# Ninety-six token slots per expert in place of 128, with 128-column stationary operands kept

## The reference, cut to what matters

```python
D_MODEL = 1024; SEQ = 256; D_FF = 3584; N_EXPERTS = 8; TOP_K = 2

def moe_ffn(h, router, w_gate_up, w_down):
    B, S, D = h.shape
    t = h.reshape(B * S, D)
    logits = (t @ router).astype(jnp.float32)
    top_v, top_i = lax.top_k(logits, TOP_K)
    gates = jax.nn.softmax(top_v, axis=-1)
    combine = jnp.sum(jax.nn.one_hot(top_i, N_EXPERTS, dtype=jnp.float32) * gates[..., None], axis=1)
    out = jnp.zeros_like(t)
    for e in range(N_EXPERTS):
        out = out + combine[:, e:e + 1].astype(t.dtype) * swiglu(t, w_gate_up[e], w_down[e])
    return out.reshape(B, S, D)
```

## Time and profile before

| | |
|---|---|
| median of 3 runs | 1419.13 us (1418.8 to 1419.32) |
| span of the profiled execution | 1417.7 us |
| TensorE busy | 1411.1 us (100% of the span), 6721 matmuls |
| TensorE weight loads | 1185.2 us (84%) |
| VectorE busy | 1234.8 us (87%) |
| ScalarE busy | 964.5 us (68%) |
| GpSimd busy | 101.9 us (7%) |
| HBM traffic | 442.93 MB, 312 GB/s over the span |

### The profile page before, as it was taken

One profiled execution on the slowest core, in us unless ns is written; L12 is line 12 of the kernel. 1 busy time (PEld: TensorE's weight loads), 2 busy tenths in 40 slices (PEclk: granted clock), 3 DMA queues, 4 the chain that ended last, 5 costly groups with the idle time before them and its releaser, 6 DMA issues.

```text
span 1417.7 us, 19898 instructions
## 1 busy us (share of the span) xinstructions
PE 1411.1 (100%) x6721; PEld 1185.2 (84%) x6721; DVE 1234.8 (87%) x1207; ACT 964.5 (68%) x840; POOL 101.9 (7%) x147
## 2 busy tenths in 40 slices
PE   9999999999999999999999999999999999999999
PEld 8998888888988888888888888888888888888887
DVE  6486888878677898999989999999999999999887
ACT  7465544443694677777777777787777777777775
POOL 4010000000022020010010000001001000000000
PEclk9999999999999999999999999999999999999999
DMA  9554655564445799999999999999999999999995
GB/s 321 163 180 147 219 196 178 178 204 144 127 177 194 274 384 389 375 378 393 379 382 394 374 374 396 394 374 382 393 371 382 395 382 374 395 383 382 383 393 195
DMA packets 212592, 442.93 MB, mean 312 GB/s; under 512 B 16372, under 2 KB 56760, under 8 KB 212544
## 3 DMA queue, kind: packets, MB, share of 16 engines
q1 hardware_dynamic: 208640, 430.18, 83.0%
q0 software_dynamic: 3888, 12.13, 2.9%
q10 hardware_dynamic: 16, 0.00, 0.0%
HBM read 434.88 MB, written 7.37 MB: 312 GB/s over the span
## 4 chain that ended last, share of the span: by engine, by line
PE 98%; ACT 1%; DVE 1%; issue 0%; POOL 0%; ACTq 0%; DVEq 0%; POOLq 0%
PE PS L1729 21%; PE PS L1730 21%; PE PS L1733 21%; PE PS L1431 5%; PE PS L1430 5%; PE PS L1432 5%; PE PS L1162 3%; PE PS L1218 2%; PE PS L1210 2%; PE PS L1212 2%; PE PS L1269 1%; PE PS L1275 1%; PE PS L1272 1%; PE PS L1718 1%; PE PS L1192 1%; PE PS L1721 1%
## 5 line engine op out<-in xcount | busy, mean ns | idle before, releaser
L1884 DVE TENSOR_TENSOR wlo<-ring,whi 128x2048 fp32r<-128x2048 f32 x334 | 758.8, 2290 | 53.3 <-ACT whi L799 51.2
L799 ACT ACTIVATE whi<-ring 128x2048 fp32r<-128x2048 f32 x334 | 639.8, 1918 | 184.3 <-PE PS L1733 173.8
L1729 PE MATMUL PS<-whi,xhi 128*128 128x512 f32 x864 | 340.8, 394 | 0.0
L1730 PE MATMUL PS<-whi,xlo 128*128 128x512 f32 x864 | 336.6, 390 | 0.0
L1733 PE MATMUL PS<-wlo,xhi 128*128 128x512 f32 x864 | 231.0, 389 | 0.0
L1733 PEld LDWEIGHTS PS<-wlo,xhi 128*128 128x128 f32 x864 | 162.1, 188 | 34.0 <-DVE wlo L1884 0.2
L1730 PEld LDWEIGHTS PS<-whi,xlo 128*128 128x128 f32 x864 | 162.4, 188 | 32.4
L1729 PEld LDWEIGHTS PS<-whi,xhi 128*128 128x128 f32 x864 | 162.3, 188 | 32.4
L1729 PE MATMUL PS<-whi,hhi 128*128 128x512 f32 x440 | 171.4, 389 | 0.0
L1730 PE MATMUL PS<-whi,hlo 128*128 128x512 f32 x440 | 171.2, 389 | 0.0
L1733 PE MATMUL PS<-wlo,hhi 128*128 128x512 f32 x440 | 117.8, 390 | 0.0
(11 more groups left out here) (387 smaller groups left out, 1637.1 us busy)
## 6 DMA issues: line engine op xcount, KB each, us to landing
ring<-in_moe_w_gate_up SPq DMA_DIRECT2D x448, 512.0 KB, 6.7
ring<-in_moe_w_down SPq DMA_DIRECT2D x224, 512.0 KB, 7.2
ring<-in_dense_w_gate_up SPq DMA_DIRECT2D x56, 512.0 KB, 4.6
ring<-in_dense_w_down SPq DMA_DIRECT2D x28, 512.0 KB, 4.1
ring<-in_a_w_in SPq DMA_DIRECT2D x12, 768.0 KB, 8.6
ring<-in_mem_w_kv SPq DMA_DIRECT2D x4, 1024.0 KB, 7.7
ring<-in_a_w_out SPq DMA_DIRECT2D x4, 1024.0 KB, 5.3
ring<-in_b_w_out SPq DMA_DIRECT2D x4, 1024.0 KB, 7.3
```

Of the source, the lines that this page charges most:

```text
L799: nc.scalar.activation(whi[:, j, :], ring[:, h * SLOT:(h + 1) * SLOT], ACT.Copy).then_inc(S("highs"), 1)
L1729: mm(out_, lhsT=xh, rhs=whi[:, j, c0:c0 + HD], start=begin, stop=False)
L1730: mm(out_, lhsT=xl, rhs=whi[:, j, c0:c0 + HD], start=False, stop=False)
L1884: v.tensor_tensor(wlo[:, j, :], ring[:, h * SLOT:(h + 1) * SLOT], whi[:, j, :].bitcast(F32), ALU.subtract).then_inc(S("lows"), 1)
```

## The change

`CAP` becomes 96, so a pass gives each expert 96 slots and `PASSES` becomes 3. The stationary operands of the matmuls stay 128 columns wide: they are read through `wide_` and `hhiW`/`hloW`, patterns that take the 96 slots and the 32 columns behind them, and write all 128 partitions of the accumulators, of which 96 are then read. Everything else that goes by slots becomes 96 wide: the moving identity of the transposes, the one-hot gather, the hidden splits, the row fetches and adds, and the squares of `turn_rows` (12 in place of 16, three per block). The placing of slots gets a step for a third pass.

```diff
-CAP = 128
+CAP = 96
...
-        Sx = carve(o, NT, CAP); o += NT * CAP
+        Sx = carve(o, NT, P); o += NT * P
...
-        xe_ = slice(0, CAP)
+        xe_, wide_ = slice(0, CAP), slice(0, P)
+        hhiW, hloW = ([bass.AP(h.tensor, h.offset + c * CAP, [list(h.ap[0]), [1, P]]) for c in range(4)] for h in (hhiE, hloE))
...
-            pool.tensor_copy(blank[:, :, 1], iota[0:NC + 1]).then_inc(S("iota"), 1)
+            pool.tensor_copy(blank[:, :, 1], iota[0:NC + 1, 0:CAP]).then_inc(S("iota"), 1)
...
-                    last = mm(PS[:, 6 + k // KH, (k % KH) * CAP:(k % KH + 1) * CAP], lhsT=xn[:, t, k * P:(k + 1) * P], rhs=Sx[:, t, :],
+                    last = mm(PS[:, 6 + k // KH, (k % KH) * CAP:(k % KH + 1) * CAP], lhsT=xn[:, t, k * P:(k + 1) * P], rhs=Sx[:, t, 0:CAP],
...
-                        (PS[0:CAP, expert_bank(i, b) + g, :], xhi[:, 2 * q + kk, xe_], xlo[:, 2 * q + kk, xe_], kk * D + g * EB, q == 0 and kk == 0,
+                        (PS[:, expert_bank(i, b) + g, :], xhi[:, 2 * q + kk, wide_], xlo[:, 2 * q + kk, wide_], kk * D + g * EB, q == 0 and kk == 0,
...
-                        (PS[0:CAP, 4 + hh, :], hhiE[:, 2 * (q - 4) + kk, :], hloE[:, 2 * (q - 4) + kk, :], kk * D + hh * HD,
+                        (PS[:, 4 + hh, :], hhiW[2 * (q - 4) + kk], hloW[2 * (q - 4) + kk], kk * D + hh * HD,
...
-                        y_last = three(PS[0:CAP, 4 + hh, :], xhi[:, c, xe_], xlo[:, c, xe_], whi[:, j, c0:c0 + HD], wlo[:, j, c0:c0 + HD],
+                        y_last = three(PS[:, 4 + hh, :], xhi[:, c, wide_], xlo[:, c, wide_], whi[:, j, c0:c0 + HD], wlo[:, j, c0:c0 + HD],
...
+                for q in range(2, PASSES):
+                    then(v.tensor_scalar(over_at, place_at[:, 0], float(q * CAP), float((NE - 1) * CAP), ALU.is_ge, ALU.mult))
+                    then(v.tensor_tensor(place_at[:, 2], place_at[:, 2], over_at, ALU.add))
...
-                        part = v.tensor_scalar(Sx[:, t], iota, put_at[:, t:t + 1], None, ALU.is_equal)
+                        part = v.tensor_scalar(Sx[0:CAP, t], iota[0:CAP], put_at[:, t:t + 1], None, ALU.is_equal)
...
-                    (r, c), last = divmod(n, 4), n == 15
+                    (r, c), last = divmod(n, 4), n == CAP // 8 - 1
...
-                        turn_rows(range(4 * (b - 2), 4 * (b - 1)))
+                        turn_rows(range(CAP // 32 * (b - 2), CAP // 32 * (b - 1)))
...
-                return v.tensor_scalar(Sx[:, t], first_slot, key[:, t:t + 1], None, ALU.is_equal)
+                return v.tensor_scalar(Sx[:, t, 0:CAP], first_slot[:, 0:CAP], key[:, t:t + 1], None, ALU.is_equal)
```

More of the change, by code:

```diff
@@ L59, in build @@
     PASSES = -(-SEQ // CAP)
-    assert CAP <= P
+    assert CAP <= P and CAP % 32 == 0
     x_d, mem_d = T["x"][0], T["mem"][0]
@@ L292, in build @@
         o = 2 * NT * FB
-        Sx = carve(o, NT, CAP); o += NT * CAP
+        Sx = carve(o, NT, P); o += NT * P
         tok_f = carve(o, NT); o += NT
         gate, gate_next = carve(o, 1)[0:CAP], carve(o + 1, 1)[0:CAP]; o += 2
-        xe_ = slice(0, CAP)
+        xe_, wide_ = slice(0, CAP), slice(0, P)
+        hhiW, hloW = ([bass.AP(h.tensor, h.offset + c * CAP, [list(h.ap[0]), [1, P]]) for c in range(4)] for h in (hhiE, hloE))
         NC = PASSES * NE
-        iota = carve(o, CAP); o += CAP
-        iotai = arena[:, o:o + CAP].bitcast(I32); o += CAP
+        iota = carve(o, P); o += P
+        iotai = arena[:, o:o + P].bitcast(I32); o += P
         m8 = carve(o, NT, 8); o += NT * 8
@@ L305, in build @@
         picked = carve(o, NT + 1, NE); o += (NT + 1) * NE
-        first_slot = carve(o, CAP); o += CAP
+        first_slot = carve(o, P); o += P
         key = carve(o, NT); o += NT
@@ L310, in build @@
         place_at = carve(o, 3, 2 * NT); o += 6 * NT
+        over_at = carve(o, 2 * NT); o += 2 * NT
         place_i = arena[:, o:o + 2 * NT].bitcast(I32); o += 2 * NT
@@ L663, in _ @@
             pool.wait_ge(S("att_out"), 1)
-            pool.iota(iotai, pattern=[[1, CAP]], base=0, channel_multiplier=0).then_inc(S("iota"), 1)
+            pool.iota(iotai, pattern=[[1, P]], base=0, channel_multiplier=0).then_inc(S("iota"), 1)
             pool.wait_ge(S("iota"), 1)
@@ L672, in _ @@
             pool.memset(blank[:, :, 0], 0.0).then_inc(S("iota"), 1)
-            pool.tensor_copy(blank[:, :, 1], iota[0:NC + 1]).then_inc(S("iota"), 1)
-            pool.tensor_scalar(blank[:, :, 2], iota[0:NC + 1], float(SEQ), None, ALU.add).then_inc(S("iota"), 1)
+            pool.tensor_copy(blank[:, :, 1], iota[0:NC + 1, 0:CAP]).then_inc(S("iota"), 1)
+            pool.tensor_scalar(blank[:, :, 2], iota[0:NC + 1, 0:CAP], float(SEQ), None, ALU.add).then_inc(S("iota"), 1)
             pool.wait_ge(S("iota"), 8)
@@ L1942, in turn_rows @@
                 for n in squares:
-                    (r, c), last = divmod(n, 4), n == 15
-                    done = v.transpose(xsT[32 * c:32 * c + 32].rearrange("p k (q s) -> p k q s", q=4)[:, :, r, :],
+                    (r, c), last = divmod(n, 4), n == CAP // 8 - 1
+                    done = v.transpose(xsT[32 * c:32 * c + 32].rearrange("p k (q s) -> p k q s", s=32)[:, :, r, :],
                                        xs[32 * r:32 * r + 32].rearrange("p (k q f) -> p k q f", k=KD, q=4)[:, :, c, :])
```

## The result

The changed kernel takes 1422.74 us (median of 10 runs, 1422.14 to 1423.0) against 1419.18 us before (10 runs, 1418.38 to 1419.61): a ratio of 1.0026, with a 95% interval of 1.0016 to 1.0035. I had forecast 1414.5 us, faster by 0.33%.

A forecast was written before the change was run, and what follows sets the result against it. TensorE's stream was taken as the bound. Only transposes gained, 4.6 us: 1417.7 - 4.6 = 1413.1 us of span, with runs 1.4 us above it, so 1414.5 us; range 1412.6 to 1416.9.

The forecast's parts named there:

- What bounds the kernel: Expert stage: TensorE's own stream, 117.5 us per expert, sets the time; relief of other engines gives nothing.
- The transposes: Expert groups of four: 96 moving columns cut the pace from 110 to 84 ns, three gains per group.
- The fourth: Last transpose of each group, before an fp32r matmul's load: keeps 110 ns; rival that all four gain, 6.0 us, chance 0.18.
- The term of 4.6 us: Transpose gain: 4.4 us in the expert groups plus 0.2 us in turning the second expert's tokens.
- The big matmuls: Expert matmuls with 512 moving columns: pace stays 0.227 us despite hidden patterns starting every 96 columns; 0 us.
- weight of 18 to 1: Sign of a wrong prediction: a changed big-matmul pace would weigh 18 times as much per nanosecond as the transposes.
- 0.03 for anything slower: Chance given to a second pass (2355 us) or something slower not seen.
- Gather, routing, DMA, VectorE: First expert's gather keeps 0.111 us, routing steps are hidden, DMA neither gives nor takes, VectorE falls to 93%; 0 us.
- 547 by my slope: VectorE's hidden subtraction at 384 columns, from 684 ns at 512 and 1.07 ns a column: 0.14 us less each.
- the added step: Routing: one more one-element step ahead of the pass count, about 0.2 us, hidden behind TensorE's gather with 1 us to spare.

The follow-up runs named there:

- the last fence above: The 96-slot kernel with hidden chunks 128 columns apart, its stationary operands made 96 columns wide with outputs on 96 partitions: 1425.18 us, ratio 1.0039.
- 128-column-pitch version: The changed 96-slot kernel, but with the hidden operand's four chunks 128 columns apart and not 96: 1415.0 us, ratio 0.9967 to the kernel before.

## Why the prediction was wrong

**What bounds the kernel: right.** TensorE's stream set the time in every version, and no other engine's relief or load moved it.

**The transposes: right.** 84 ns forecast, and 0.33 us for four in the chain (0.082 each). The fourth gains nothing, as I had it: the chain books 0.33 instead of 0.36 on the transposes, but 0.03 more on the matmul behind them, whose load has become visible. With a 96-column load behind it (the last fence above) the matmul after the transposes takes 0.23 us and not 0.26, so there the fourth gains as well: it was that load. The term of 4.6 us is confirmed by the 128-column-pitch version: 1415.0 against 1419.2 to 1419.4 us, 4.2 to 4.4 us, with 1414.5 forecast for a kernel whose large matmuls keep their pace. That also speaks against the rule of the Trainium skill, "TensorE: Matmul & The Clock Gate" (LDWEIGHTS), that a load lasts its columns over 1.2 GHz, as a limit on transposes: with 128 stationary columns they go at 82 ns, not 107.

**The step that failed: "The big matmuls ... The four patterns of the hidden operand now start every 96 columns ... I take no cost ... 0 us."** I had seen the new starts, had no row for them, and set the cost to zero because a slower load should be covered by the 227 ns of the matmul. The cover does not work that way. Where stationary reads start at another place within 512 bytes than the moving read, a matmul's pace is 4 to 6 ns longer, although the records of the loads stay at 188 ns and lie well within the matmul. Over the 24 matmuls of a block, with three of four chunks shifted, the mean is 5.8 ns, and 56 blocks make 7.8 us. The term that was set to 0 us measures 7.8 us. I named a changed pace of the large matmuls as what would make the prediction wrong, with its weight of 18 to 1, and gave it no chance of its own beyond the 0.03 for anything slower; the range had no room for it.

**And there was a row.** The trace before has the same thing on a small scale, 232 to 235 ns for the matmuls on `memhl` (1.87 us for eight, above). I had read their mean of 396 to 402 ns beside the others' 389 and not asked why.

**Gather, routing, DMA, VectorE: right, and worth nothing.** The gather keeps its pace of 0.111 us: 24 matmuls in 2.82 us with 96 moving columns and 2.84 with 128.

```profile
466.41 2.82 PE L1691 MATMUL PS<-arena,xn 128*128 128x96 f32 x24
```

The hidden subtraction takes 551 ns (547 by my slope), and the stretch from 465 to 582 us has TensorE as busy as before (117.10 against 117.14 us): the added step is hidden. There are still seven fetches, hence one pass.

**What stays open.** Why the distance between the two starts matters: a shared read path whose turns fall badly would fit, but nothing here shows one. Why matmuls on a well-placed chunk stay slow behind others, and why 18 shifted reads in a block cost as much as 24, is open too. Distances of 4, 32, 128 and 384 bytes were slow by themselves, those of 8, 12 and 256 only in company with others. Of the distances tried only multiples of 512 were fast, and none had a pace under 227 ns.

## What to carry to other kernels

When a tile is packed tighter, its operands' starts move, and on an engine that is 100% busy a few nanoseconds in thousands of matmuls outweigh what the packing saves: in matmuls like these (fp32r, 512 moving columns, a load before each) keep the stationary chunks a multiple of 512 bytes apart and on the same place within 512 bytes as the moving operand, even if that leaves gaps. Look at the memory map for such distances before any change, and compare like groups in the trace: a group of equal shape whose mean is 5 ns longer is a finding. A step that the prediction sets to zero because "it is covered" needs a row that shows the cover, or a price in the range.

## What the runs showed of the hardware

- 512-column fp32r matmuls start 227 ns apart when the stationary and the moving read begin at the same place within 512 bytes, and 231 to 233 ns apart otherwise, on average, with single steps from 224 to 241 ns. It is relative: 128 bytes on all tiles cost nothing (1418.57 us), 128 bytes on the weights alone 29 us (1448.1 us).
- Transposes with a 128-column stationary operand start 110 ns apart with 128 moving columns, 82 with 96 and 69 with 4.
- A 96-column stationary operand makes a 512-column matmul slower (230 ns against 227) although its load record is shorter (161 ns against 188).
